# First FFN: seven products of 256 columns in its second up chunk, in place of eight of 512

## The reference

```python
def conv_ffn(n, w_up, conv_w, conv_b, w_down):          # first FFN, d_ff = 2816
    S = n.shape[1]
    u, g = jnp.split(n @ w_up, 2, axis=-1)
    pad = CONV_WIDTH // 2
    gp = jnp.pad(g, ((0, 0), (pad, pad), (0, 0)))
    gc = sum(gp[:, j:j + S] * conv_w[j] for j in range(CONV_WIDTH)) + conv_b
    return (jax.nn.silu(gc) * u) @ w_down

def swiglu(x, w_gate, w_up, w_down):                    # the other four
    return (jax.nn.silu(x @ w_gate) * (x @ w_up)) @ w_down
```

## Time and profile before

| what | value |
|---|---|
| median of 3 runs | 2705.03 us (2704.81 to 2705.25) |
| the profiled execution, its own time | 2704.6 us |
| its span on the core | 2702.8 us |
| granted TensorE clock, mean | 1.00 |
| busy: PE, DVE, ACT, POOL | 99%, 79%, 40%, 18% |

### The profile page before, as it was taken

One profiled execution on the slowest core, in us unless ns is written; L12 is line 12 of the kernel. 1 busy time (PEld: TensorE's weight loads), 2 busy tenths in 40 slices (PEclk: granted clock), 3 DMA queues, 4 the chain that ended last, 5 costly groups with the idle time before them and its releaser, 6 DMA issues.

```text
span 2702.8 us, 39460 instructions
## 1 busy us (share of the span) xinstructions
PE 2683.3 (99%) x16008; PEld 2364.8 (87%) x16008; DVE 2123.5 (79%) x2137; ACT 1073.9 (40%) x1175; POOL 495.2 (18%) x304
## 2 busy tenths in 40 slices
PE   9999999999999999999999999999999999999999
PEld 7978679888999889999767899998999988899998
DVE  6778866459999889888576988889888775698885
ACT  4333634444444463333364533335333332343332
POOL 0124124041000241001233100013000142500000
PEclk9999999999999999999999999999999999999999
DMA  4221133322322323223312222233222332222332
GB/s 170 80 76 64 50 110 125 109 71 85 110 97 107 112 93 108 100 104 109 114 35 73 95 98 107 97 112 107 101 102 96 107 112 106 94 94 95 109 107 96
DMA packets 39763, 266.24 MB, mean 99 GB/s; under 512 B 4528, under 2 KB 5808, under 8 KB 8240
## 3 DMA queue, kind: packets, MB, share of 16 engines
q1 hardware_dynamic: 38016, 259.02, 27.1%
q10 hardware_dynamic: 1584, 4.87, 0.5%
HBM read 261.77 MB, written 2.10 MB: 98 GB/s over the span
## 4 chain that ended last, share of the span: by engine, by line
PE 71%; DVE 4%; POOL 1%; issue 1%; ACT 1%; DVEq 0%; POOLq 0%; ACTq 0%
PE ps L2125 23%; PE ps L2127 23%; PE ps L2126 23%; DVE w_lo L1088 1%; PE ps L2726 1%; POOL ssum L1971 0%; POOL up_b L1977 0%; PE ps L2738 0%; PE ps L2765 0%; DVE up_b L1221 0%; POOL up_b L2000 0%; ACT w_hi L550 0%; POOL sq L1969 0%; DVE q_h L1794 0%; DVE h L1238 0%
## 5 line engine op out<-in xcount | busy, mean ns | idle before, releaser
L550 ACT ACTIVATE w_hi<-stage 128x2048 fp32r<-128x2048 f32 (+1 forms) x241 | 412.0, 1710 | 488.2 <-PE ps L2127 485.7
L2125 PE MATMUL ps<-x_hi,w_hi 128*128 128x512 f32 (+1 forms) x1656 | 574.7, 347 | 0.7 <-DVE w_lo L1291 0.6
L2127 PE MATMUL ps<-x_hi,w_lo 128*128 128x512 f32 (+1 forms) x1656 | 565.7, 342 | 0.0
L2126 PE MATMUL ps<-x_lo,w_hi 128*128 128x512 f32 (+1 forms) x1656 | 565.6, 342 | 0.0
L1088 DVE TENSOR_TENSOR w_lo<-stage,w_hi 128x2048 fp32r<-128x2048 f32 (+1 forms) x241 | 499.0, 2070 | 39.3 <-ACT w_hi L550 39.0
L2000 POOL TENSOR_TENSOR up_b<-up_b,gate_b 128x1024 f32<-128x1024 f32 x50 | 114.3, 2286 | 1303.2 <-PE ps L2127 1212.3
L2125 PEld LDWEIGHTS ps<-x_hi,w_hi 128*128 128x128 f32 x1656 | 314.2, 190 | 39.1 <-issue 3.1
L2126 PEld LDWEIGHTS ps<-x_lo,w_hi 128*128 128x128 f32 x1656 | 314.2, 190 | 37.2 <-issue 3.1
L2127 PEld LDWEIGHTS ps<-x_hi,w_lo 128*128 128x128 f32 x1656 | 314.0, 190 | 36.3
L2125 PE MATMUL ps<-f_hi,w_hi 128*128 128x512 f32 x880 | 342.9, 390 | 0.0
L2126 PE MATMUL ps<-f_lo,w_hi 128*128 128x512 f32 x880 | 342.9, 390 | 0.0
(11 more groups left out here) (454 smaller groups left out, 5068.4 us busy)
## 6 DMA issues: line engine op xcount, KB each, us to landing
stage<-in_stream SPq DMA_DIRECT2D x242, 1024.0 KB, 4.8
h<-in_x ACTq DMA_DIRECT2D x2, 1024.0 KB, 5.3
out_x<-h SPq DMA_DIRECT2D x8, 256.0 KB, 2.1
h<-in_x SPq DMA_DIRECT2D x6, 256.0 KB, 3.8
mem_raw<-in_mem ACTq DMA_DIRECT2D x1, 1024.0 KB, 4.8
stage<-in_stream SPq DMA_DIRECT2D x6, 128.0 KB, 4.0
h<-in_x SPq DMA_DIRECT2D x1, 512.0 KB, 5.7
mask_f<-in_constants ACTq DMA_DIRECT2D x1, 448.0 KB, 6.2
```

The lines of the kernel that those rows point to most:

```text
L550: act.activation(w_hi[slot][:, 0:width], stage[slot][:, 0:width], ACT.Copy).then_inc(hi_ready, 1)
L2125: pe.matmul(out_ap, wh, xh, start=first, stop=False)
L2126: pe.matmul(out_ap, wh, xl, start=False, stop=False)
L2127: return pe.matmul(out_ap, wl, xh, start=False, stop=last)
```

## The change

One entry of the table: up 1 of the first FFN (chunk 3) goes from `eight` to `seven_products`.

```diff
-SEVENS = [{"gate": range(2, STEPS), "up": range(2, STEPS)}] + [{"gate": range(2, STEPS), "up": range(2 if i == 0 else 1, STEPS)} for i in range(4)]
+SEVENS = [{"gate": range(2, STEPS), "up": range(1, STEPS)}] + [{"gate": range(2, STEPS), "up": range(2 if i == 0 else 1, STEPS)} for i in range(4)]
```

## The result

| | before | after |
|---|---|---|
| median, 11 runs each | 2705.09 us (2704.70 to 2705.73) | 2712.03 us (2711.53 to 2713.21) |
| the profiled execution, its own time | 2704.6 | 2712.4 |
| its span | 2702.8 | 2710.6 |
| TensorE idle, span less busy | 19.5 | 25.3 |

The ratio of the medians is 1.0026, with a 95% interval of 1.0017 to 1.0034: 7 us slower. The forecast was 2711.8.

A forecast was written before the change was run, and what follows sets the result against it. The DVE's list up to chunk 7's `w_lo` was taken to set TensorE's pace: 6.90 - 0.14 + 0.06 = 6.82 us later, 6.81 by TensorE's waits, so 2711.8 us from a 2705.0 median; range 2708.8 to 2714.0.

The forecast's parts named there:

- The bound: TensorE busy 2683.3 of 2702.8 us, but at chunk 7 it already waits for the DVE's `w_lo`, 0.39 us.
- TensorE's 0.80: Chunk 3 on TensorE: 48 matmuls in 10.88 us become 84 in 10.08, 0.80 us less.
- DVE, 6.90 added and idle time -0.14: DVE list up to chunk 7's `w_lo`: 6.90 us more work, idle time changing by minus 0.14.
- The wait for `s_hi`: Chunk 3's new `s_lo` on the DVE waits for ACT's `s_hi`, as chunk 5's does: plus 0.32 us.
- Silu to taking out: DVE starts taking chunk 3 out 1.44 us after ACT's Silu starts, in place of 1.19: plus 0.25.
- POOL's turn: POOL's product for up 0 holds a DVE sum ahead of chunk 3's `w_lo`: 1.69 or 1.81 us, taken as plus 0.06.
- POOL once more: Rival: POOL asks 0.43 us earlier and holds chunk 7's `w_lo` for 1.8 us, giving 2713.6; chance 0.10.
- The clock: Rival: the gap before chunk 5 halves the granted clock, kernel taking up to 2720 us; chance 0.06.
- Its own sign of being wrong: Forecast is wrong if a granted clock below 1.00 stands in the windows of chunks 5 to 7.
- the wait before chunk 7: TensorE waits 1.67 us there for `w_lo`, covering up to 3.3 us of time at half clock.
- the case of no effect: Rival: the change does nothing, though DVE and ACT lists show new instructions; chance 0.01.
- a faster kernel: Faster by over 0.2%: no mechanism, since 0.80 + 0.39 us is the most; chance 0.01.

The follow-up runs named there:

- dummy: Kernel before, with useless DVE additions (6.35 us) where the change puts its work; 2711.60 us, ratio 1.0024.
- room_before: Kernel before, with outer convolution taps of gates 0 to 2 and POOL's products for up 0 and 1 on 8 of 512 columns; 2704.37 us.
- room_after: Changed kernel, with outer convolution taps of gates 0 to 2 and POOL's products for up 0 and 1 on 8 of 512 columns; 2703.66 us.
- fill: Changed kernel with 30 unused matmuls of 256 columns in the gap before chunk 5; 2712.10 us, run once more 2711.81.
- early: Changed kernel with chunk 5's weight sums moved on the DVE into its wait for the Silu of gate 1; 2710.05 us.
- again: Changed kernel as it is, run once more beside the one with the gap before chunk 5 filled; 2711.79 us.
- nopool: Changed kernel with POOL's product for up 0 on only 8 of 512 columns; 2710.46 us.
- poolsums: Changed kernel with chunk 3's four weight sums made by POOL in place of the DVE; 2712.12 us.

## Why the prediction was right

- **The bound.** Read from TensorE's one wait: the DVE already paced it at chunk 7. `dummy` showed it by DVE work alone (6.35 us of work, 6.6 us longer), `room_before` and `room_after` by the other sign once the DVE had room.
- **TensorE's 0.80.** Measured as 0.80 in the rows of the `room` pair. In the changed kernel it becomes waiting.
- **DVE, 6.90 added and idle time -0.14.** The `w_lo` of chunk 7 moved by 6.98 (681.70 - 0.19 - 674.53), against 6.82. What was short: the first sum of chunk 4 starts 2.40 after `s_lo`, not 2.20 (635.48 to 637.88), since it waits until the DVE's own `s_lo` is written (`s_f`, which it overwrites, is read by it). The row it was priced by stands before an instruction that has no such wait. The wait for `s_hi` was 0.31 (0.32 forecast), Silu to taking out 1.46 (1.44).
- **POOL's turn.** It fell on the last sum of chunk 3, as forecast, and cost 1.69 as before, so the 0.06 was not needed.
- **POOL once more** (0.10). In after it asks at 684.35, behind `w_lo`. In `fill` it asks at 681.97, during `w_lo` (681.48 to 683.23), and `w_lo` still takes 1.75: it is POOL that waits, 3.12 in place of 2.00 us. `early` shows the same (asked at 680.02, 3.39 us long, a `w_lo` of 1.75). By the Trainium skill (SBUF — State Buffer, "Who interferes with whom") the port pair that the two engines share is an exclusive lock, and the order of issue decides who blocks; these rows agree. The case in which POOL asks ahead of this `w_lo` did not come up.
- **The clock** (0.06). Here the prediction misjudged the chance, though hardly the time. It named the gap before chunk 5, found no row for what such a gap does, and gave the fall little weight; the clock fell in all 21 executions of the changed kernel on record. Its own sign of being wrong, a granted clock below 1.00 in the windows of chunks 5 to 7, did appear. The price was right in kind: it had said that the wait before chunk 7, 1.67 by its sum and 1.61 measured, covers a fall. Its rate was a little high: at the lower clock a matmul of 256 columns takes 0.213 in place of 0.12, so such time loses 44% of itself and not half. That the fall was over early in chunk 5, and so nearly all covered, nothing in the prediction foretold: that the time came out within 0.3 us of the forecast is in this part luck. The Trainium skill (TensorE: Matmul & The Clock Gate, "Why this matters for your kernels") warns of such gaps, and the trace agrees; had this rule been weighed higher, the forecast of the time would have been no better.
- **The total.** 6.98 from the DVE's list, with 0 from the clock in the typical execution, on 2705.09 is 2712.1; measured 2712.03 and 2711.79.
- **The chances.** With 0.01 each for the case of no effect and for a faster kernel they add up to 1.01; nothing hangs on it.

## What to carry to other kernels

Find the next place where the list of some other engine already holds up the bounding one, and add up what the edit does to that engine's whole list to there. Here 0.8 us less on TensorE cost 6.9 us on a DVE whose average load of 79% hid a stretch with hardly any slack, and the waits at the chunks between did not matter. Moving work to an idle engine gave it all back, since its reads slowed the busy one down; moving it into a wait of the same engine gained 2 us. A gap in TensorE's work may also cost clock, and that is paid only as far as the next wait doesn't cover it.

## What the runs showed of the hardware that was not expected

- A gap of TensorE of 3.8 us before chunk 5 was followed by the lower clock in every execution of after, `again`, `nopool` and `poolsums`; the gap of `dummy`, 3.10 in its profile, in seven of nine. (The mean clock of an execution is given to 0.001: by an estimate, half the clock for less than 2.7 of 2710 us would not show in it. The two with 1.000 took 2711.60 and 2712.30, no less than the others.) Gaps of 0.3 to 1.7 us (`early`, `fill`, chunks 3 and 4) never were. At 1.2 GHz matmuls of 256 columns start 0.213 apart, at 2.4 GHz 0.12.
- A gap of the same 3.81 us cost different amounts: in after the clock was down for the last 2 us of the gap (0.76 over the 4 us from 656.80), in `again` only from the start of chunk 5 on, and 2.16 against 1.51 us were lost.
- A product of POOL that takes 2.00 us beside a DVE instruction with one SBUF input took 3.49 (after), 5.69 and 9.77 (`dummy`) when the DVE ran instructions with two SBUF inputs back to back. It need not get in at the first boundary between two of them: in `dummy` it waited through eight, and got in ahead of the last sum of chunk 4. In after it asked 0.26 behind the start of the first sum of chunk 3 and got in ahead of the fourth, but 0.25 behind the start of the first sum of chunk 5 (654.94) and got in ahead of the second, which took 2.49. Why it gets in at one boundary and not at another stays open.
